# Query strips in the even layer, expert panels parted by contraction, and one panel queued ahead of a barrier

## The chip, the cores and the metric

The kernel runs on one core of one Trainium2 chip. The metric is device time in microseconds (us) of one execution. The inputs lie in the chip's main memory (HBM), and the outputs are written back there.

## The reference

Two layers of a decoder trunk are computed for 256 prompt tokens and 8 sequences of 4 new tokens, 288 tokens in all, in f32. Layer 0 ("even") is gated linear attention in chunks of 16 tokens beside a pooling mixer; layer 1 ("odd") is retention. Each mixer is followed by a mixture of 64 experts, of which every token takes 8. The two parts that the change touches are these (cut from the reference):

```python
# even layer, one chunk of 16 tokens: state query plus attention inside the chunk
q_in = qc * jnp.exp(b)
k_in = kc * jnp.exp(-b)
o_inter = jnp.einsum('bchk,bhkv->bchv', q_in, S)
att = jnp.einsum('bthk,bshk->bhts', q_in, k_in)      # then masked to s <= t
o_intra = jnp.einsum('bhts,bshv->bthv', att, vc)
S_new = jnp.exp(b_last[:, 0])[..., None] * S + jnp.einsum('bshk,bshv->bhkv', k_dec, vc)
return S_new, o_inter + o_intra

# experts: w_exp_gate and w_exp_up are 1024 x 256, w_exp_down is 256 x 1024
h = jax.nn.silu(xt @ wg) * (xt @ wu)
acc = acc + gcol[:, None] * (h @ wd)
```

The even layer has 4 heads with keys of 64 and values of 128, so a chunk's state is 64 x 128 for each head. Each new sequence has a state of its own.

## The kernel before, in words

**Even layer.** Features lie on the partitions. The queries `QI` are stored with two heads to a set of 128 partitions: for f (pair of heads) and k (head of the pair) the 64 rows of head k hold the query and the other 64 hold zeros, so one matmul against a state pair `SS[:, f, i, :]` (two heads stacked, 128 x 128) answers for one head at a time. L901 does this for the 15 chunks that have an earlier state: the state is the stationary operand (128 x 128, loaded anew for each matmul) and 32 query columns move past it (2 heads x 16 tokens). L907 does it for the 8 sequences' states `gs0` with 8 moving columns each. Both accumulate into the PSUM banks of the groups `oT` (prompt) and `oTs` (samples), which stay open while L912 (the pooling mixer's `pool` groups) runs; L919 and L924 then add the attention inside the chunks (`V` against the masked scores `AT`) and close them. L931 sums squares for the norm, and L1158, L1162 and L1116 are the output projection behind it. ScalarE copies `oT` and `oTs` out (L1541, L1450).

**Banks.** `group_order` lists every PSUM group of the program; `plan_groups` gives them the 8 banks in turn (7 in turn in the odd layer), and around the expert loop by a fixed table. A group waits until the group before it in its bank has been copied out.

**Weight panels.** The SP queue loads weights in panels of 2 MB into a ring of 6 slots (`wait_slot`, `expert_panel`). For a pair of experts panel 0 holds gate and up of the first expert, panel 1 those of the second, panel 2 the down weights of both. One pair, the last of the 32 (`HOME`), is loaded ahead of the loop into its own place in the arena (`HOME_UP`, `HOME_DOWN`) and computed in the middle of the loop, as the 17th; it is called the parked pair here. The first two pairs fill the ring before the loop. Between them the queue also issues the router's weights (`WR`), the parked pair's gate and up, then waits for a barrier of the four compute engines (`phase_end`, L750), and loads `PIN` (the layer's embedding input), the shared expert's down weights (`WSD`) and the rest of the ring.

**Expert loop.** For each pair PE does gate and up (`gate_up`, L1252, 16 matmuls, the two experts in the two column halves of the array), transposes the next pair's token rows (L1245), scatters the last pair's outputs (L1228, L1224), transposes the hidden values (L1259) and does down (L1266). Gate and up wait for panels 0 and 1 both. Panel 0 and 1 of the pair after next are issued when `gate_up` has ended (`bank_full[0]`), since they take the same slots. The token rows of each pair are gathered by an indirect DMA from `x_rows`.

## Time and profile before

| | us |
|---|---|
| median of 3 runs | 1671.39 (1671.09 to 1671.58) |
| the profiled execution's own time | 1670.99 |
| its span, first to last instruction | 1669.2 |
| PE busy in the span | 1587.6 (95%) |
| PE weight loads (PEld) busy | 799.2 (48%) |
| VectorE (DVE) busy | 539.7 (32%) |
| ScalarE (ACT) busy | 341.4 (20%) |
| GpSimd (POOL) busy | 144.6 (9%) |
| mean granted TensorE clock, share of full | 0.983 |

The chain of work that ended last is made up of PE for 81% of the span, DMA for 11%, DVE for 3%. The expert loops take about two thirds of the span: the first runs from 210 to 699 us, the second from 1129 to 1616 us.

A row of a window reads: start:end, its length, then the busy time and the count of instructions of PE, PEld, DVE, ACT and POOL, then the granted clock of PE (1.00 is full), the mean busy share of the 16 DMA engines, and the GB/s that they moved. A row of a timeline reads: start in us, duration in us, engine, line of the kernel, operation, output <- input, shapes, count (x), and in brackets how long the engine had been idle before it and who ended the wait. SPq is the queue of SyncE that issues DMAs; its duration is the issuing alone. A matmul in f32 shows as two records, so 30 matmuls are x60. A row of DMA issues ends in the median time from issue to landing.

### The profile page before, as it was taken

The page shows a single profiled execution, that of the slowest core. Times are in us where ns is not written, and L with a number is a line of the kernel's source. Part 1 is how long each engine was busy: PE and PEld are TensorE (multiplying, and loading weights), DVE is VectorE, ACT ScalarE, POOL GpSimd, SP SyncE. Part 2 cuts the span into 40 slices and gives each one's busy share as a digit, 9 for nine tenths or more (in the row PEclk, how much of TensorE's full clock was granted, in tenths as well). Part 3 has the DMA queues.
Part 4 walks back from the last instruction along what each step waited for, and adds up shares of the span by engine and source line. Part 5 has one row for each costly group of instructions (what it writes and reads, how often), then busy time and mean ns, then how long its engine had stood idle before and what let it go on. Part 6 is the DMA issues. An engine that isn't in the chain of part 4 may idle for free.

```text
span 1669.2 us, 21844 instructions
## 1 busy us (share of the span) xinstructions
PE 1587.6 (95%) x7954; PEld 799.2 (48%) x7954; DVE 539.7 (32%) x1322; ACT 341.4 (20%) x693; POOL 144.6 (9%) x221
## 2 busy tenths in 40 slices
PE   8999899999999999999999999989999999999998
PEld 5784544334344433446665755554443434443343
DVE  2145722222222222261434245372222222222225
ACT  2102122121122221231222222012212112221122
POOL 0330100000000000000011111010000000000000
PEclk9969999999999999999999999989999999999999
DMA  9623779999989999955385586577999998999970
GB/s 299 245 82 133 277 313 419 421 421 420 420 348 421 420 420 420 388 200 188 134 269 195 196 279 235 202 310 306 421 421 421 420 419 362 420 421 419 421 291 29
DMA packets 119271, 536.09 MB, mean 321 GB/s; under 512 B 17849, under 2 KB 29369, under 8 KB 69408
## 3 DMA queue, kind: packets, MB, share of 16 engines
q1 hardware_dynamic: 95975, 470.35, 70.5%
q0 software_dynamic: 21360, 61.64, 10.2%
q10 hardware_dynamic: 1872, 3.22, 0.6%
q8 instruction: 44, 0.72, 0.2%
q14 instruction: 20, 0.16, 0.0%
HBM read 526.15 MB, written 23.87 MB: 330 GB/s over the span
## 4 chain that ended last, share of the span: by engine, by line
PE 81%; DMA 11%; DVE 3%; issue 2%; ACT 1%; SPq 1%; POOL 0%; ACTq 0%; DVEq 0%
PE ps L1252 23%; PE ps L1116 12%; PE ps L1094 12%; DMA weights<-in_w_exp_up 11%; PE ps L1266 10%; PE ps L1228 5%; PE ps L1245 3%; PE ps L1224 2%; PE ps L1259 1%; PE ps L1010 1%; PE ps L1105 1%; PE ps L1286 1%; PE ps L988 1%; PE ps L901 1%; PE ps L1001 1%
## 5 line engine op out<-in xcount | busy, mean ns | idle before, releaser
L1252 PE MATMUL ps<-weights,x_feat 128*64 128x512 f32 x1984 | 437.8, 593 | 36.8 <-DMA weights<-in_w_exp_up 18.5
L1252 PEld LDWEIGHTS ps<-weights,x_feat 128*64 128x64 f32 x1984 | 147.1, 137 | 320.9 <-issue 318.2
L1266 PE MATMUL ps<-weights,arena 128*64 128x512 f32 x992 | 226.5, 598 | 0.9 <-ACT arena L1450 0.9
L1094 PE MATMUL ps<-x_feat,weights 128*128 128x288 f32 x832 | 210.2, 411 | 1.1 <-ACT x_feat L1450 1.1
L1094 PEld LDWEIGHTS ps<-x_feat,weights 128*128 128x128 f32 x832 | 159.9, 194 | 45.1 <-issue 3.8
L2104 DVE CAST split<-state 128x1024 fp32r<-128x1024 f32 (+1 forms) x66 | 44.7, 678 | 324.9 <-ACT state L1450 324.9
L2101 DVE SCALAR_TENSOR_TENSOR arena<-arena,ps 128x256 f32<-128x256 f32 x64 | 30.7, 480 | 365.3 <-ACT arena L1679 365.3
L2423 POOL DMA_INDIRECT arena<-x_rows,arena x64 | 63.6, 993 | 891.0 <-DVE arena L2094 845.9
L1450 ACT ACTIVATE state<-ps 128x512 f32<-128x512 f32 x132 | 78.8, 597 | 268.5 <-PE ps L1266 261.1
L1116 PE MATMUL ps<-weights,x_feat 128*128 128x512 f32 x288 | 126.7, 594 | 3.0 <-ACT x_feat L1476 3.0
L1266 PEld LDWEIGHTS ps<-weights,arena 128*64 128x64 f32 x992 | 65.7, 136 | 132.3 <-issue 130.9
L1679 ACT ACTIVATE arena<-ps 128x256 f32<-128x256 f32 x64 | 24.5, 383 | 444.6 <-PE ps L1252 444.6
L1228 PE MATMUL ps<-split,token_rows 128*128 128x512 f32 x256 | 111.8, 437 | 1.6 <-DVE y_low L2107 1.6
L1450 ACT ACTIVATE arena<-ps 128x256 f32<-128x256 f32 (+7 forms) x150 | 59.0, 405 | 222.4 <-PE ps L1116 84.5
L1228 PE MATMUL ps<-y_low,token_rows 128*128 128x512 f32 x256 | 100.8, 394 | 0.0
L1116 PEld LDWEIGHTS ps<-weights,x_feat 128*128 128x128 f32 x288 | 54.1, 190 | 69.8 <-issue 64.5
L1245 PEld LDWEIGHTS ps<-const,arena 128*128 128x128 f32 x512 | 62.3, 194 | 51.1 <-issue 51.1
L1116 PE MATMUL ps<-weights,arena 128*128 128x512 f32 x192 | 84.3, 592 | 0.0
L1450 ACT ACTIVATE x_feat<-ps 128x512 f32<-128x512 f32 x137 | 74.0, 588 | 49.8 <-PE ps L1245 45.9
L2107 DVE TENSOR_TENSOR y_low<-state,split 128x1024 fp32r<-128x1024 f32 (+1 forms) x66 | 78.7, 1193 | 2.3
L1245 PE MATMUL ps<-const,arena 128*128 128x128 f32 x512 | 74.4, 288 | 0.0
L1116 PEld LDWEIGHTS ps<-weights,arena 128*128 128x128 f32 x192 | 36.1, 190 | 41.6 <-issue 41.1
(289 smaller groups left out, 1280.8 us busy)
## 6 DMA issues: line engine op xcount, KB each, us to landing
weights<-in_w_exp_gate SPq DMA_DIRECT2D x124, 1024.0 KB, 14.8
weights<-in_w_exp_up SPq DMA_DIRECT2D x124, 1024.0 KB, 18.8
weights<-in_w_exp_down SPq DMA_DIRECT2D x124, 1024.0 KB, 16.9
weights<-in_w_in_c SPq DMA_DIRECT2D x24, 1024.0 KB, 8.1
arena<-in_state_ret POOLq DMA_DIRECT2D x20, 512.0 KB, 5.5
out_ret_sample<-arena POOLq DMA_DIRECT2D x20, 512.0 KB, 6.5
weights<-in_w_in_a SPq DMA_DIRECT2D x8, 1024.0 KB, 10.9
weights<-in_w_ple_gate SPq DMA_DIRECT2D x8, 1024.0 KB, 17.8
```

What stands on the lines that cost most here:

```text
L1094: last = pe.matmul(ps[:, 0:T], lhs(c), XT[:, c, :], start=(c == 0), stop=(c == n - 1))
L1116: last = pe.matmul(ps[0:r, 0:w], lhs(c), rhs(c), start=(c == 0), stop=(c == n - 1))
L1224: last = pe.matmul(PS[TS * q:TS * q + TS, 7, 0:256], TOK[u][:, SEQ:T].bitcast(F32), YF[:, 256 * q:256 * q + 256], start=False, stop=stop, ...
L1228: last = pe.matmul(bank((f"sum{l}", j, n)), TOK[u][:, P * j:P * j + P], y[:, 512 * n:512 * n + 512], start=False, stop=stop and y is YLO, ...
L1245: last = pe.transpose(ps[:, c * P:c * P + P], xc[:, 4 * q + c, :], ident)
L1252: last = pe.matmul(ps[64 * s:64 * s + 64, :], XGT[u][:, c, 64 * s:64 * s + 64], rhs, start=(c == 0), stop=(c == KC - 1))
L1266: last = pe.matmul(ps[64 * s:64 * s + 64, :], HT[u][:, c, 64 * s:64 * s + 64], wd[s][:, c, 512 * n:512 * n + 512], start=(c == 0), stop=(c ...
L1450: return act.activation(dst, src, ACT.Copy, **k)
L2101: return STT(HH[u], HS[u], META[u][:, 0:1], PS[:, 0, DE:2 * DE], ALU.mult, ALU.mult)
L2104: return dve.tensor_copy(YHI[:, c], YF[:, c])
L2107: return TT(YLO[:, c], YF[:, c], YHI[:, c].bitcast(F32), ALU.subtract)
L2423: pool.indirect_dma_start(XG[u], None, xd, bass.IndirectOffsetOnAxis(ap=GI[u], axis=0), bounds_check=last_row, oob_is_err=False).then_inc( ...
```

## The change

Three edits are made together.

1. **Query strips.** The roles in the state query are swapped: a chunk's 32 query columns are the stationary operand and the state moves past it, 128 columns. Four chunks write the four 32-row strips of a bank (L923 for the prompt, 16 chunks with the first one's state zeroed by a new memset; L930 for the 8 sequences, whose stationary columns hold the tokens of 4 sequences, 3 of them masked later). ScalarE copies three banks out (`QS` in `state`, `QSS` in `keys`, the latter scaled by the mask column `own_strip`). New matmuls turn them back to feature order and add them to `oT` (L949, against the identity) and `oTs` (L959, against `fold_all`, which sums the strips). `QI` is laid out by chunks, and three groups (`qS` twice, `qSs`) join `group_order`, so every later group's bank moves on by three.
2. **Panels parted by contraction.** For the first pair and the last pair of each loop, panel 0 holds the first half of the contraction (rows of gate and up) of both experts and panel 1 the second half (`contraction_panel`; 4 KB a piece where it was 8 KB). `gate_up_halves` waits for panel 0 alone, does 8 of the 16 matmuls, then waits for panel 1. After the first pair's first half it raises `half_consumed`, and the queue waits for that instead of for the end of `gate_up` before it issues the third pair's panel 0.
3. **One panel ahead of the barrier.** The second pair's panel 0 is issued before the queue's wait for `phase_end`, instead of behind it, `PIN` and `WSD`.

PE's program in the even layer: L901 and L907 are the state queries, L912 the pooling, L919 and L924 the attention, L931 the norm. Before:

```order
L855 MATMUL ps<-arena,side 64x128 x32
L901 MATMUL ps<-arena 128x2x16 x30
L907 MATMUL ps<-arena,ln_rows 128x2x4 x16
L912 MATMUL ps<-arena 128x288 x4
L919 MATMUL ps<-x_feat,arena 128x128 x8
L924 MATMUL ps<-x_feat,arena 128x32 x4
L931 MATMUL ps<-x_feat,small 128x512 x2
```

And the same place now (L877 is the former L855, L936 the former L912, L966 the former L931):

```order
L877 MATMUL ps<-arena,side 64x128 x32
L923 MATMUL ps<-arena 32x128 x32
L930 MATMUL ps<-ln_rows,arena 32x128 x16
L936 MATMUL ps<-arena 128x288 x4
L944 MATMUL ps<-x_feat,arena 128x128 x4
L949 MATMUL ps<-const,state 128x4x2x16 x4
L944 MATMUL ps<-x_feat,arena 128x128 x4
L949 MATMUL ps<-const,state 128x4x2x16 x4
L954 MATMUL ps<-x_feat,arena 128x32 x4
L959 MATMUL ps<-const,arena 128x2x16 x4
L966 MATMUL ps<-x_feat,small 128x512 x2
```

46 matmuls with a 128 x 128 stationary operand have become 48 with a 128 x 32 one, and 12 that turn the results have been added in front of the norm.

SP's queue between the parked pair's panels and the loop, first layer. Before, the panel of the second pair stands behind the barrier's wait, `in_p_prompt` and `in_w_sh_down`:

```order
L734 DMA arena<-in_w_exp_gate 128x2048
L734 DMA arena<-in_w_exp_up 128x2048
L622 DMA arena<-in_p_prompt 128x2x256 [waits phase_end]
L623 DMA arena<-in_p_sample 32x256
L755 DMA state<-in_w_sh_down 128x1024
L755 DMA arena<-in_w_sh_down 128x1024
L734 DMA weights<-in_w_exp_gate 128x2048 [waits bank_full_7]
L734 DMA weights<-in_w_exp_up 128x2048
L734 DMA weights<-in_w_exp_gate 128x2048 [waits bank_full_7]
L734 DMA weights<-in_w_exp_up 128x2048
```

Now:

```order
L738 DMA arena<-in_w_exp_gate 128x2048
L738 DMA arena<-in_w_exp_up 128x2048
L738 DMA weights<-in_w_exp_gate 128x2048 [waits bank_full_2]
L738 DMA weights<-in_w_exp_up 128x2048
L626 DMA arena<-in_p_prompt 128x2x256 [waits phase_end]
L627 DMA arena<-in_p_sample 32x256
L768 DMA state<-in_w_sh_down 128x1024
L768 DMA arena<-in_w_sh_down 128x1024
L738 DMA weights<-in_w_exp_gate 128x2048 [waits bank_full_2]
L738 DMA weights<-in_w_exp_up 128x2048
```

Two transfers of 1 MB each have moved ahead of the wait for the barrier; the bank that the slot's wait names is another one because the banks moved on by three.

SP's queue at the head of the loop now (before, the first transfer here waited for `bank_full_0` too, inside a counted loop):

```order
L782 TENSOR_LOAD small [waits flag_ready]
L782 ISA x2
L738 DMA weights<-in_w_exp_gate 128x2048 [waits half_consumed]
L738 DMA weights<-in_w_exp_up 128x2048
L738 DMA weights<-in_w_exp_gate 128x2048 [waits bank_full_0]
L738 DMA weights<-in_w_exp_up 128x2048
L738 DMA weights<-in_w_exp_down 128x2048 [waits bank_full_1]
```

Only the third pair's panel 0 has the new wait; its panels 1 and 2 wait as before.

The diff, cut to its core:

```diff
             g.extend(("dS", 2, f, i) for f in range(2) for i in range(2))
+            g.extend((("qS", 0), ("qS", 1), ("qSs",)))
+            g.extend(("pool", f) for f in range(4))
             g.extend((("oT", 0), ("oT", 1), ("oTs",)))
-            g.extend(("pool", f) for f in range(4))
...
+                def contraction_panel(num, e0, k):
+
+                    s = slot_full[num % SLOTS]
+                    dst = wp(num).rearrange("p (s m x) -> p s m x", s=2, m=2)
+                    for m, w in enumerate((A["w_exp_gate"], A["w_exp_up"])):
+                        src = w[l, e0:e0 + 2].rearrange("e (p c) n -> p e (c n)", c=KC)
+                        sp.dma_start(dst[:, :, m, :], src[:, :, 1024 * k:1024 * k + 1024]).then_inc(s, 16)
+
...
+                        if NUM[(f"shgu{l}",)] + 5 == n0 + 3 * pr + k:
                             sp.wait_ge(phase_end, 4 * (2 * l + 1))
...
                         wait_slot(n0 + 3 * pr + k)
-                        expert_panel(n0 + 3 * pr + k, 2 * pr, k)
+                        if pr == 0 and k < 2:
+                            contraction_panel(k + n0, 0, k)
+                        else:
+                            expert_panel(n0 + 3 * pr + k, 2 * pr, k)
...
-                def two_pairs(it, late):
-                    for u in range(1 if isinstance(it, int) else 2):
+                def two_pairs(it, late, pairs=2):
+                    for u in range(pairs):
                         for k in range(3):
                             if k == 2:
                                 sp.wait_ge(bank_full[1], base[1] + 3 * (u - 1 + late) + 6 * it)
+                            elif isinstance(it, int) and it == 1 and u + k == 0:
+                                sp.wait_ge(sem("half_consumed"), l + 1)
                             else:
                                 sp.wait_ge(bank_full[0], base[0] + 2 * (u + late) - 3 + 4 * it)
-                            expert_panel(n0 + 3 * u + k, 4 * it + 2 * u, k)
-
-                with sp.Fori(1, HOME // 2 + 1) as it:
+                            if isinstance(it, int) and it > 1 and k < 2:
+                                contraction_panel(n0 + 6 * it + k, 4 * it, k)
+                            else:
+                                expert_panel(n0 + 3 * u + k, 4 * it + 2 * u, k)
+
+                two_pairs(1, 0, 2)
+                with sp.Fori(2, HOME // 2 + 1) as it:
                     two_pairs(it, 0)
                 with sp.Fori(HOME // 2 + 1, PAIRS // 2 - 1) as it:
                     two_pairs(it, 1)
-                two_pairs(PAIRS // 2 - 1, 1)
+                two_pairs(PAIRS // 2 - 1, 1, 1)
...
+            pe.wait_ge(sem("const_in"), 16)
             for f in range(2):
-                out2 = begin(("oT", f)).rearrange("p (k t) -> p k t", k=2)
-                outs.append(out2)
-                for i in range(1, NCA):
-                    pe.matmul(out2[:, :, CA * i:CA * i + CA], SS[:, f, i, :], QI[:, f, :, CA * i:CA * i + CA],
-                              start=(i == 1), stop=False, skip_group_check=True)
-            out4 = begin(("oTs",))[:, 0:H * TS].rearrange("p (h t) -> p h t", h=H)
+                ps = begin(("qS", f))
+                for i in range(NCA):
+                    q, g = i % 4, i // 4
+                    last = pe.matmul(ps[TS * q:TS * q + TS, P * g:P * g + P], QI[:, f, i].rearrange("p k c -> p (k c)"), SS[:, f, i, :],
+                                     start=(g == 0), stop=(g == 3), skip_group_check=True)
+                end(last, ("qS", f))
+            ps = begin(("qSs",))
             for f in range(2):
                 for i in range(NSEQ):
-                    c = DSEQ * i
-                    pe.matmul(out4[:, 2 * f:2 * f + 2, c:c + DSEQ], gs0[:, f, i, :], QI[:, f, :, SEQ + c:SEQ + c + DSEQ],
-                              start=(f == 0 and i == 0), stop=False, skip_group_check=True)
+                    q, g = i % 4, 2 * f + i // 4
+                    last = pe.matmul(ps[TS * q:TS * q + TS, P * g:P * g + P], QI[:, f, NCA + i // 4].rearrange("p k c -> p (k c)"), gs0[:, f, i, :],
+                                     start=(g == 0), stop=(g == 3), skip_group_check=True)
+            end(last, ("qSs",))
...
+                out2 = begin(("oT", f)).rearrange("p (k t) -> p k t", k=2)
                 for k in range(2):
                     h = 2 * f + k
                     for j in range(2):
-                        last = pe.matmul(outs[f][:, k, P * j:P * j + P], V[:, j, P * h:P * h + P],
-                                         AT[:, h, P * j:P * j + P], start=False, stop=(k == 1 and j == 1),
-                                         skip_group_check=True)
+                        pe.matmul(out2[:, k, P * j:P * j + P], V[:, j, P * h:P * h + P], AT[:, h, P * j:P * j + P],
+                                  start=(k == 0 and j == 0), stop=False, skip_group_check=True)
+                emptied(pe, ("qS", f))
+                for g in range(4):
+                    tokens_of = out2[:, :, 64 * g:64 * g + 64].rearrange("p k (i c) -> p i k c", c=CA)
+                    last = pe.matmul(tokens_of, QS[f][:, P * g:P * g + P], ident, start=False, stop=(g == 3),
+                                     skip_group_check=True)
                 end(last, ("oT", f))
+            out4 = begin(("oTs",))[:, 0:H * TS].rearrange("p (h t) -> p h t", h=H)
             for h in range(H):
-                last = pe.matmul(out4[:, h, :], V[0:TS, 2, P * h:P * h + P], AT[0:TS, h, SEQ:T],
-                                 start=False, stop=(h == H - 1), skip_group_check=True)
+                pe.matmul(out4[:, h, :], V[0:TS, 2, P * h:P * h + P], AT[0:TS, h, SEQ:T], start=(h == 0), stop=False,
+                          skip_group_check=True)
+            emptied(pe, ("qSs",))
+            for f in range(2):
+                for g in range(2):
+                    last = pe.matmul(out4[:, 2 * f:2 * f + 2, CA * g:CA * g + CA], QSS[:, P * (2 * f + g):P * (2 * f + g) + P],
+                                     fold_all[:, 0:TS], start=False, stop=(f == 1 and g == 1), skip_group_check=True)
             end(last, ("oTs",))
...
+                def gate_up_halves(u, ring, it, ps):
+                    for k in range(2):
+                        n = ring + k
+                        pe.wait_ge(slot_full[n % SLOTS], 32 * (n // SLOTS + 1) + 32 * it)
+                        w = wp(n).rearrange("p (s m c n) -> p s m c n", s=2, m=2, c=4)
+                        for c in range(4):
+                            for s in range(2):
+                                last = pe.matmul(ps[64 * s:64 * s + 64, :], XGT[u][:, 4 * k + c, 64 * s:64 * s + 64],
+                                                 w[:, s, :, c, :], start=(k == 0 and c == 0), stop=(k == 1 and c == 3))
+                        if it == 0 and k == 0:
+                            last.then_inc(sem("half_consumed"), 1)
+                    return last
...
-                        else:
+                        elif not (first or last):
                             for n in range(ring, ring + 2):
                                 pe.wait_ge(slot_full[n % SLOTS], 32 * (n // SLOTS + 1) + 32 * it)
                         pe.wait_ge(bank_free[0], base[0] + uses(0, pr, 0))
-                        gate_up(u, HOME_UP if home else [wp(ring), wp(ring + 1)], PS[:, 0, :]).then_inc(bank_full[0], 1)
+                        if first or last:
+                            gate_up_halves(u, ring, it, PS[:, 0, :]).then_inc(bank_full[0], 1)
+                        else:
+                            gate_up(u, HOME_UP if home else [wp(ring), wp(ring + 1)], PS[:, 0, :]).then_inc(bank_full[0], 1)
...
+                    for f in range(2):
+                        full(act, ("qS", f))
+                        st.free(copy(QS[f], bank(("qS", f))), ("qS", f))
+                    full(act, ("qSs",))
+                    act.wait_ge(sem("even_table"), 16)
+                    st.free(copy(QSS, bank(("qSs",)), scale=own_strip), ("qSs",))
...
+            st.run(pool.memset(SS[:, :, 0, :], 0.0))
+            st.after
```

## Rows read from the trace of the kernel before

**Rows 1.** Windows in the first expert loop: engines, PEclk, DMA share, GB/s.

```profile
350.00:400.00 50.00, 46.02 (x244) 20.10 (x241) 11.87 (x32) 9.95 (x20) 2.97 (x3) 1.00 1.02 421
```

**Rows 2.** Timeline of the SP queue, first expert loop: weight panels issued.

```profile
217.32 0.35 SPq L734 DMA_DIRECT2D weights<-in_w_exp_gate  x1
...
223.68 0.80 SPq L734 DMA_DIRECT2D weights<-in_w_exp_down  x2
...
230.71 0.33 SPq L734 DMA_DIRECT2D weights<-in_w_exp_gate  x1
...
245.26 0.33 SPq L734 DMA_DIRECT2D weights<-in_w_exp_gate  x1
...
318.37 0.33 SPq L734 DMA_DIRECT2D weights<-in_w_exp_gate  x1
...
447.32 0.33 SPq L734 DMA_DIRECT2D weights<-in_w_exp_gate  x1
```

**Rows 3.** Timeline of PE, first and last pair of the expert loops.

```profile
210.05 7.09 PE L1252 MATMUL ps<-weights,x_feat 128*64 128x512 f32 x32 [1.13 <-ACT x_feat L1450]
...
681.64 7.09 PE L1252 MATMUL ps<-weights,x_feat 128*64 128x512 f32 x32 [1.62 <-issue]
...
1598.93 7.09 PE L1252 MATMUL ps<-weights,x_feat 128*64 128x512 f32 x32 [1.49 <-issue]
```

**Rows 4.** Windows: DMA before the loop's first panel and beside the parked pair.

```profile
212.00:216.00 4.00, 4.00 (x20) 1.56 (x18) 0.00 (x0) 0.00 (x0) 0.00 (x0) 1.00 0.00 0
...
472.00:476.00 4.00, 4.00 (x20) 1.15 (x16) 0.12 (x1) 0.00 (x0) 0.00 (x0) 1.00 0.16 65
```

**Rows 5.** Timeline of PE, the even layer's state queries and what follows.

```profile
103.69 13.01 PE L901 MATMUL ps<-arena 128*128 128x32 f32 x60
116.51 6.97 PE L907 MATMUL ps<-arena,ln_rows 128*128 128x8 f32 x32
123.33 4.19 PE L912 MATMUL ps<-arena 128*128 128x288 f32 x8
127.31 2.75 PE L919 MATMUL ps<-x_feat,arena 128*128 128x128 f32 x16
130.00 1.07 PE L924 MATMUL ps<-x_feat,arena 32*128 32x32 f32 x8
131.00 2.21 PE L931 MATMUL ps<-x_feat,small 128*128 128x512 f32 x6
```

**Rows 6.** Windows: PEclk in those queries, behind them, and in the output projection.

```profile
100.00:105.00 5.00, 5.00 (x43) 4.67 (x39) 2.18 (x12) 0.00 (x0) 0.00 (x0) 0.50 0.00 0
...
125.00:130.00 5.00, 5.00 (x23) 4.17 (x21) 1.99 (x4) 0.79 (x2) 0.00 (x0) 0.60 0.00 0
...
133.00:161.00 28.00, 28.00 (x71) 12.69 (x71) 15.74 (x18) 2.65 (x5) 0.00 (x0) 1.00 0.48 191
```

**Rows 7.** Timeline of PE at full clock: strips, wide matmuls, transposes.

```profile
47.89 1.96 PE L1111 MATMUL ps<-weights,x_feat 128*32 128x128 f32 x64
...
79.47 7.93 PE L1094 MATMUL ps<-x_feat,weights 128*128 128x288 f32 x32
...
160.51 1.04 PE L1082 MATMUL ps<-const,x_tok 128*128 128x128 f32 x8
```

**Rows 8.** The second layer's barrier: windows, SP timeline, DMA issues, PE timeline.

```profile
1085.00:1090.00 5.00, 1.70 (x10) 0.95 (x8) 3.79 (x10) 1.36 (x5) 0.00 (x0) 0.81 0.69 285
...
1090.32 0.38 SPq L622 DMA_DIRECT2D arena<-in_p_prompt  x1
...
arena<-in_p_prompt SPq DMA_DIRECT2D x1, 256.0 KB, 2.6
...
1098.15 0.74 PE L1186 MATMUL ps<-const,arena 128*128 128x128 f32 x4
```

**Rows 9.** Timeline of PE and DVE behind the first layer's shared matmuls.

```profile
198.54 0.32 PE L1216 MATMUL ps<-arena 128*128 128x12 bf16 x3 [0.55 <-DVE arena L2083]
...
199.01 0.44 DVE L2052 TENSOR_TENSOR arena<-arena,ps 128x288 f32<-128x288 f32 x1
```

More of the change, by code:

```diff
@@ L130, in constants @@
             ((p[:, None] // DSEQ) == np.arange(8)[None, :]) * 1.0,
-            np.tile(inv.reshape(-1), (P, 1))]
+            np.tile(inv.reshape(-1), (P, 1)), (p[:, None] % CA // DSEQ == p[:, None] // TS) * 1.0]
     f = np.float32
@@ L399, in trunk @@
         invc = ce.take(64)
+        own_strip = ce.take(1)
         gate_ops = a.take(8 * RANK + 256 + T)
@@ L413, in trunk @@
         EB = a.take(2 * T).rearrange("p (f t) -> p f t", f=2)
-        QI = a.take(4 * T).rearrange("p (f k t) -> p f k t", f=2, k=2)
+        QI = a.take(4 * T).rearrange("p (f i k c) -> p f i k c", f=2, k=2, c=CA)
         EN = LX
@@ L430, in trunk @@
         AT = XTb[:, 4 * T:8 * T].rearrange("p (h t) -> p h t", h=4)
+        QS = [STATE[:, 512 * f:512 * f + 512] for f in range(2)]
+        QSS = keys[:, 0:512]
         a = Cut(AR[:, :], ASZ)
@@ L887, in even_pe @@
                 for j, (o, r) in enumerate(CH):
-                    last = pe.matmul(ps[0:r, o:o + r], KI[:, h // 2, o:o + r], QI[:, h // 2, h % 2, o:o + r],
-                                     start=True, stop=True)
+                    last = pe.matmul(ps[0:r, o:o + r], KI[:, h // 2, o:o + r],
+                                     QI[:, h // 2, o // CA:(o + r) // CA, h % 2, :], start=True, stop=True)
                 end(last, ("att", h))
@@ L895, in even_pe @@
             pe.wait_ge(sem("even_in"), 16 * 8)
-            outs = []
+            pe.wait_ge(sem("const_in"), 16)
             for f in range(2):
-                out2 = begin(("oT", f)).rearrange("p (k t) -> p k t", k=2)
-                outs.append(out2)
-                for i in range(1, NCA):
-                    pe.matmul(out2[:, :, CA * i:CA * i + CA], SS[:, f, i, :], QI[:, f, :, CA * i:CA * i + CA],
-                              start=(i == 1), stop=False, skip_group_check=True)
-            out4 = begin(("oTs",))[:, 0:H * TS].rearrange("p (h t) -> p h t", h=H)
+                ps = begin(("qS", f))
[5 more added lines that the diff above has]
+            ps = begin(("qSs",))
             for f in range(2):
                 for i in range(NSEQ):
-                    c = DSEQ * i
-                    pe.matmul(out4[:, 2 * f:2 * f + 2, c:c + DSEQ], gs0[:, f, i, :], QI[:, f, :, SEQ + c:SEQ + c + DSEQ],
-                              start=(f == 0 and i == 0), stop=False, skip_group_check=True)
+                    q, g = i % 4, 2 * f + i // 4
+                    last = pe.matmul(ps[TS * q:TS * q + TS, P * g:P * g + P], QI[:, f, NCA + i // 4].rearrange("p k c -> p (k c)"), gs0[:, f, i, :],
+                                     start=(g == 0), stop=(g == 3), skip_group_check=True)
+            end(last, ("qSs",))
             for g in range(4):
@@ L1792, in even_dve @@
                         dve.wait_ge(sem("queries_zeroed"), 1)
-                    st.run(STT(QI[0:64, f, 0, :], ps[0:64], DKA ** -0.5, EB[0:64, f, :], ALU.mult, ALU.mult))
-                    st.free(STT(QI[64:128, f, 1, :], ps[64:128], DKA ** -0.5, EB[64:128, f, :], ALU.mult, ALU.mult), ("qk", f))
+                    for k in range(2):
+                        rows = slice(64 * k, 64 * k + 64)
+                        ins = STT(QI[rows, f, :, k, :], ps[rows].rearrange("p (i c) -> p i c", c=CA), DKA ** -0.5,
+                                  EB[rows, f, :].rearrange("p (i c) -> p i c", c=CA), ALU.mult, ALU.mult)
+                        if k:
+                            st.free(ins, ("qk", f))
+                        else:
+                            st.run(ins)
                 else:
```

## Prediction

> **What bounds the kernel now.** I read the granted clock and the chain of waits first, then windows, then the timeline beside each edit. PE is busy for 95% of the span and holds 81% of the chain, with DMA next at 11%, so an edit is worth what it takes off PE's path, or what it takes off a transfer that PE waits for. Three stages matter.
>
> The expert loop has two regimes. In a DMA-bound window the engines move 421 GB/s at a share of 1.02, and PE is busy for 46.02 of 50 us [rows 1]. Early in the loop a pair takes 245.26 - 230.71 = 14.6 us, since PE sets the pace; from 318.37 to 447.32, eight pairs, a pair takes 16.1 us, since the transfers do [rows 2]. A panel of 2 x 1024 KB takes 2.10 MB / 421 GB/s = 5.0 us, three panels 15.0, and the other 1.1 us are left for the token rows that each pair gathers. So the loop starts with a lead of full slots, eats it up, and then waits for DMA; what starts the transfers earlier ends the first half earlier. At the parked pair the engines run dry (share 0.16 from 472 to 476) [rows 4]: the ring is full there, and the second half starts afresh, relative to PE. A gain before the parked pair is then a plain shift of all that follows, and the second half ends DMA-bound again: the last gate-and-up waits 1.62 us in layer 0 and 1.49 in layer 1 [rows 3].
>
> The even layer's state queries are PE's alone: L901 to the start of L931 take 131.00 - 103.69 = 27.3 us without a gap [rows 5], at a granted clock of 0.50, the lower of the two levels (1.2 GHz); it is back at 1.00 before 130 [rows 6].
>
> **Part 1, query strips.** Removed: 60 + 32 = 92 records, 13.0 + 7.0 = 20.0 us, 217 ns each [rows 5]. L907 moves only 8 columns and still takes 217 ns, so the load of 128 x 128 is what is paid. Added: 32 + 16 matmuls, 96 records of four-strip form. The trace has that form in L1111: 64 records in 1.96 us at full clock, 31 ns each, that is four strips side by side [rows 7]. 96 records are 2.9 us at full clock, 5.9 at half. Then the pooling: 4.19 us as before at half clock, or 8 x 248 ns = 2.0 at full [rows 5, 7]. Then 16 records of `V` against `AT` and 16 that turn `QS` back: 130 ns each at full clock [rows 7], 4.2 us, or 6.9 at half. Then L924's 8 records, 1.07, and 8 for `QSS` at 130 ns, together 2.1. ScalarE's three copies lie behind the strips and beside the pooling, where ScalarE is idle (no busy time from 100 to 105, 0.79 us from 125 to 130) [rows 6]; without that cover they would cost about 2 us.
>
> What is left is the clock. The mean of 0.60 from 125 to 130 means a rise at about 129, 5.7 us after the 288-column matmuls began at 123.33, while 20 us of 32- and 8-column matmuls before them left it at 0.50 though PE was fully busy [rows 5, 6]. If the strips (128 columns and all four column groups at work) count like wide matmuls, the clock is back when they end, and the stage takes 5.9 + 2.0 + 4.2 + 2.1 = 14.2 us, a gain of 13.1. If only the pooling counts, it is back at 109.6 + 5.7 = 115.3: pooling until 113.8, 7 records at half clock until 115.3, 25 at full (3.3), then 2.1, end at 120.7, a gain of 10.3. I take the middle, 11.7 us. Bounds: everything at full clock is 11.2 us, a gain of 16.1; strips that don't overlap at all at half clock (96 x 217 ns = 20.8) with the same late rise end at 135.6, a loss of 4.6.
>
> [...]
>
> Everything behind shifts with L931: the norm, the output projection (28.0 us of unbroken PE work from 133 to 161 [rows 6]), the barrier.
>
> **Part 2, first pair.** `half_consumed` comes half of 7.09 us after 210.05, so the third pair's panel 0 is issued at 213.8, where it was 217.32 [rows 2, 3]. The engines are idle there (share 0.00 from 212 to 216) [rows 4]. Panel 0 then ends 3.5 us earlier, and panel 1, issued at 217.3, follows without a gap (until 223.8, with the gathered rows 225.0). Panel 2 is issued at 223.68, in time, and runs until about 230.0. The next panels come only with the end of the second gate-and-up at 230.71, so about 0.8 us of the lead is lost. That leaves 3.5 - 0.8 = 2.7 us for each layer, seen from the time on at which the loop waits for DMA: 5.4 in all. Bounds: 0 (if it is lost somewhere in the ring) and 3.5 for each layer. The matmuls themselves are the same 16.
>
> **Part 2, last pair.** PE is free at 681.64 - 1.62 = 680.0, and panel 1 lands at about 681.6, so panel 0 has landed at 676.6. The first half can start at 680.0 and PE runs on through: 1.62 us saved in layer 0, 1.49 in layer 1 [rows 3], 3.1 in all. Pieces of 4 KB where there were 8: no row shows their rate alone; even 0.5 us more a panel would put panel 1 at 682.6 and the end at 682.6 + 3.5 = 686.1, still ahead of the 687.1 that PE needs. Bounds: 0 and 3.1.
>
> **Part 3, the panel ahead of the barrier.** In layer 0 DMA waits for nothing there and nobody waits for the panel: no gain. In layer 1 the panel takes its place behind the parked pair's, which keep the engines busy until about 1088.5 (share 0.69 of 1085 to 1090), so it runs until 1093.5. `PIN`, issued at 1090.32 and landed 2.6 us later until now, is behind it and lands at about 1096.1; PE wants it at 1098.15 [rows 8]. Cost 0; if the cover of 2.0 us is gone, up to 3 us. I take 0.
>
> **Moved banks.** Every group after the new three has another bank. In layer 0 the first `lists` group now follows the last shared-expert group directly in bank 0. Its matmul started at 198.54; the copy that frees the bank ends at 199.45 [rows 9], so PE and the first gather behind it come about 1 us later. In layer 1 the same conflict (on the second list) existed before and goes. I take +1.0 - 0.8 = 0, between -1 and +2.
>
> **Sum.** Against the profiled execution's own 1670.99: -11.7 - 5.4 - 3.1 + 0 = 1650.8; that execution was 0.4 below the median of the runs, so the forecast is 1651 us. By the bounds alone it would go from 1643 to 1681.
>
> **The rivals.**
> - *Strips slow or clock late.* The four strips don't overlap as in L1111, since here each also has another stationary operand, or the clock stays at half through the turning matmuls (6.9 and about 4 instead of 4.2 and 2.1). Even layer -3 instead of -11.7: 1660. For it: 20 us of busy PE did not raise the clock. Against: L1111's 31 ns, and the rise after 5.7 us of wide matmuls.
> - *The ring eats the early start.* The DMA-bound stretch is long, and a lead may vanish where slots come free late. Then only the last pair's 3.1 is left of the loops: 1656. Against: eight pairs in a row at 16.1 us leave no slack in which to lose it.
> - *More than forecast.* Full clock within the strips, and the whole 3.5 us in each loop: -16.1 - 7.0 - 3.1, 1645.
> - *Slower: the clock stays down in the output projection.* Should the denser, shorter stage leave the clock at 0.50 until the layer norm, the 28.0 us of PE work from 133 to 161 at full clock [rows 6] would double: -3 - 8.5 + 28, 1688. It decides from about 20 us of doubled work on. For it: PE at 0.50 for some 25 us while fully busy. Against: the 288-column matmuls are still there, and 512-column ones follow.
>
> **How the numbers follow.** Forecast (both parts, 1647 to 1654) 0.66; strips slow or clock late 0.12; ring 0.11; more than forecast 0.07; slower 0.02; a mix that ends near no change 0.02. The range 1646 to 1657 holds the forecast, the ring and half of the larger gain. Within 0.2% (3.3 us, about what a measurement of this kernel can tell from no change): 0.02; faster 0.95; slower 0.03.
>
> **What would show it.** PE's strips: 96 records in 3 to 6 us, L931's successor starting 10 to 13 us earlier, at about 119. The clock's rise between 108 and 116. SP's first loop panel 3.5 us after the first gate-and-up's start, and the first half of the loop shorter by 2.7 us. No DMA wait ahead of the last gate-and-up. In layer 1 no idle time of PE before the transposes of `PIN`. The prediction is wrong if the strips take over 10 us, if the distance from the first to the parked pair is unchanged, or if PE waits for `PIN`.

## The result, and the profile after

The kernel after takes 1657.34 us (median of 4 runs, 1656.74 to 1660.54); the kernel before, run beside it, 1671.24 (1670.63 to 1671.58). The ratio is 0.9921, with a 95% interval of 0.9904 to 0.9938. The forecast was 1651 with a range of 1646 to 1657: the direction was right, the forecast gain was too large by 6 us, and the time lies 0.3 us outside the range.

The page of the kernel after (busy us, share of the span, instructions; then q8, the DMA queue that fetches PE's code as shown below, with packets, MB and share):

```profile
span 1655.4 us, 21804 instructions
...
PE 1575.6 (95%) x7982; PEld 789.3 (48%) x7982; DVE 539.4 (33%) x1322; ACT 343.7 (21%) x696; POOL 144.9 (9%) x222
...
q8 instruction: 44, 0.72, 0.2%
```

**Even layer.** Timeline of PE; it answers to [rows 5]:

```profile
103.72 3.64 PE L923 MATMUL ps<-arena 128*32 128x128 f32 x64
107.13 1.93 PE L930 MATMUL ps<-ln_rows,arena 128*32 128x128 f32 x32
108.99 2.37 PE L936 MATMUL ps<-arena 128*128 128x288 f32 x8
111.20 1.05 PE L944 MATMUL ps<-x_feat,arena 128*128 128x128 f32 x8
...
114.87 1.07 PE L954 MATMUL ps<-x_feat,arena 32*128 32x32 f32 x8
115.87 1.08 PE L959 MATMUL ps<-const,arena 128*128 128x32 f32 x8
116.78 2.18 PE L966 MATMUL ps<-x_feat,small 128*128 128x512 f32 x6
```

Windows of the same stretch (PEclk follows POOL's busy time); they answer to [rows 6]:

```profile
100.00:105.00 5.00, 5.00 (x61) 4.57 (x61) 2.58 (x15) 0.00 (x0) 0.00 (x0) 0.50 0.01 3
105.00:109.00 4.00, 4.00 (x79) 3.35 (x69) 3.15 (x13) 1.19 (x2) 0.25 (x1) 0.50 0.01 2
109.00:113.00 4.00, 4.00 (x29) 3.58 (x26) 2.03 (x4) 0.69 (x1) 4.00 (x7) 0.95 0.60 122
```

From the first state query to the norm it was 27.31 us, now it is 116.78 - 103.72 = 13.06. The granted clock, still 0.50 up to 109, is back when the strips end.

**Loops.** SP's queue at the first loop's head; it answers to [rows 2]:

```profile
199.06 0.33 SPq L738 DMA_DIRECT2D weights<-in_w_exp_gate  x1
...
202.50 0.33 SPq L738 DMA_DIRECT2D weights<-in_w_exp_gate  x1
...
209.01 0.80 SPq L738 DMA_DIRECT2D weights<-in_w_exp_down  x2
...
215.88 0.33 SPq L738 DMA_DIRECT2D weights<-in_w_exp_gate  x1
```

PE's gate and up of the 17th pair (the parked one) and of the last pair, layer 0, then of the last pair of layer 1; they answer to [rows 3]:

```profile
436.76 7.04 PE L1287 MATMUL ps<-arena,x_feat 128*64 128x512 f32 x32
...
662.58 7.04 PE L1298 MATMUL ps<-weights,x_feat 128*64 128x512 f32 x32
...
1585.16 7.04 PE L1298 MATMUL ps<-weights,x_feat 128*64 128x512 f32 x32
```

The first gate and up starts at 195.38 (210.05 before, -14.67), the 17th at 436.76 (454.68, -17.92), the last at 662.58 (681.64, -19.06) and without a wait. Up to here everything is as forecast or better.

**Behind the first loop.** PE's timeline of the kernel before, the last scatter of the loop and the output projection behind it:

```profile
698.88 0.39 PE L1228 MATMUL ps<-y_low,token_rows 128*128 128x512 f32 x1
699.11 7.03 PE L1116 MATMUL ps<-weights,arena 128*128 128x512 f32 x16
706.04 1.16 PE L1082 MATMUL ps<-const,x_tok 128*128 128x128 f32 x8
```

The same place in the kernel after:

```profile
679.78 0.40 PE L1263 MATMUL ps<-y_low,token_rows 128*128 128x512 f32 x1
685.03 9.38 PE L1151 MATMUL ps<-weights,arena 128*128 128x512 f32 x16 [4.86 <-issue]
694.33 1.16 PE L1117 MATMUL ps<-const,x_tok 128*128 128x128 f32 x8
```

PE stands still for 4.86 us where it had no gap, and "issue" says that the profile shows nothing that it waited for. Then the same 8 matmuls (16 records) take 9.38 us instead of 7.03. The windows of the kernel after show why:

```profile
680.00:685.00 5.00, 0.18 (x1) 0.00 (x0) 1.20 (x3) 0.00 (x0) 0.00 (x0) 0.78 1.07 355
685.00:690.00 5.00, 4.97 (x7) 2.18 (x8) 0.00 (x0) 0.60 (x1) 0.00 (x0) 0.54 0.96 322
690.00:695.00 5.00, 5.00 (x17) 2.35 (x16) 0.97 (x2) 3.21 (x5) 0.00 (x0) 1.00 1.01 365
```

In the idle time the granted clock fell towards its lower level (1.2 GHz), and it is back at full by 690, after PE had resumed at 685. The shift of -19.10 (679.78 against 698.88) has become -11.71 (694.33 against 706.04): 7.4 us are lost here.

Beside the gap stands a packet of code. Behind the loop PE jumps over the block for overfull experts (`pe.If(go > 0)`). These inputs never run it; it has some 250 instructions, if a matmul in f32 is counted as four (its two records and their two weight loads). Between that jump and the gap's end, queue q8 moves 16 KB. Its packets around the loop's end stand in the windows 652 to 654, 682 to 684 and 684 to 686 in the kernel after:

```profile
q8 instruction: 1, 0.02, 3.4%
...
q8 instruction: 1, 0.02, 3.4%
...
q8 instruction: 1, 0.02, 3.1%
```

and at 678.1 and 702.0 in the kernel before. Ahead of the loops such a packet comes every 170 to 317 records of PE, weight loads included (10 packets and 2,402 records up to 255.4 us, kernel before). So q8 feeds PE, and a packet (0.72 MB / 44 = 16 KB) is taken here as a page of code of about 250 instructions.

### The profile page after: what moved, and what is told of

Same layout as the page of the kernel before. It is cut to its first block, busy times and chain, and to the rows that moved or that the text cites. A ratio compares the mean times of both kernels' runs of the same rounds, so it can differ in the third digit from the quotient of the medians.

```text
span 1655.4 us, 21804 instructions
## 1 busy us (share of the span) xinstructions
PE 1575.6 (95%) x7982; PEld 789.3 (48%) x7982; DVE 539.4 (33%) x1322; ACT 343.7 (21%) x696; POOL 144.9 (9%) x222
## 4 chain that ended last, share of the span: by engine, by line
PE 83%; DMA 10%; DVE 3%; issue 2%; ACT 1%; SPq 1%; POOL 0%; ACTq 0%; DVEq 0%
PE ps L1287 22%; PE ps L1151 13%; PE ps L1129 12%; PE ps L1314 11%; DMA weights<-in_w_exp_up 10%; PE ps L1263 6%; PE ps L1280 3%; PE ps L1259 2%; PE ps L1298 2%; PE ps L1307 1%; PE ps L1045 1%; PE ps L1140 1%; PE ps L1334 1%; PE ps L1023 1%; PE ps L1036 1%
## 5 line engine op out<-in xcount | busy, mean ns | idle before, releaser
L1287 PE MATMUL ps<-weights,x_feat 128*64 128x512 f32 x1856 | 409.7, 593 | 27.6 <-DMA weights<-in_w_exp_up 14.6
L1287 PEld LDWEIGHTS ps<-weights,x_feat 128*64 128x64 f32 x1856 | 140.3, 137 | 291.0 <-issue 286.5
```

Of the source, the lines that this page charges most:

```text
L1287: last = pe.matmul(ps[64 * s:64 * s + 64, :], XGT[u][:, c, 64 * s:64 * s + 64], rhs, start=(c == 0), stop=(c == KC - 1))
```

## The experiments

There were two theories at the start. *Code*: PE waits for its own instructions at the jump's target, since 14 more matmuls in the even layer have moved the places where pages of code end. *Transfer*: PE waits for the projection's panel, issued at 655.32, or for a semaphore, as a consequence of the earlier panels.

**1. The blocks left out.** In the kernel after, for SP, PE, ACT and DVE:

```diff
-                with pe.If(go > 0):
+                if False:
```

> The kernel after, without the four blocks that compute experts with more tokens than fit (one for each of SP, PE, ACT and DVE, behind each expert loop; with these inputs the flag is 0 and the blocks are jumped over). Left out is that work and the jump. Theory (code): behind the first loop PE waits 4.9 us for its own instructions beyond the jump (685.03, released by nothing that the profile shows) and the low clock that follows costs 2.3 us more. Without the blocks there is nothing to jump over, so the stage from the end of the last down (680.2) to the end of L1151 is about 7 us shorter, the gap is under 1 us, and the whole kernel takes about 1650 us. Rival (transfer): PE waits for the panel of the projection, issued at 655.3; then the gap stays at 4 to 5 us and the time at 1657.

Measured: 1650.71 us (one run; before 1669.68 beside it). The last scatter starts at 681.34, and the projection follows it without a gap and at full speed:

```profile
681.57 7.03 PE L1151 MATMUL ps<-weights,arena 128*128 128x512 f32 x16
```

The projection's panel is issued at 656.86 here, 24.5 us ahead of the last scatter as in the kernel after, and PE doesn't wait for it. So the transfer theory is out, unless the block did something else as well.

**2. Empty instructions.** `for _ in range(64): pe.nop()` at the head of PE's program.

> The kernel after with 64 empty instructions at the start of PE's program, where PE waits for its inputs anyway; all that follows lies 64 instructions later in memory. Theory (code): where the instruction fetch falls relative to the jump sets the stall, so the 4.9 us ahead of L1151 change by more than 1 us (vanish, or grow), and the time with them (1650 if they vanish). Rival (transfer or a semaphore): 4.9 us as before, 1657.

> The kernel after with 128 empty instructions at the start of PE's program. Theory (code): the stall ahead of L1151 differs from 4.9 us in this kernel or in the one with 64, and may appear behind the second loop instead. Rival (transfer or a semaphore): 4.9 us in both, 1657.

> The kernel before with 56 empty instructions at the start of PE's program, about as many as the change adds to PE ahead of the first loop's end. Theory (code): the growth of PE's program alone brings the stall, so a gap of about 5 us appears ahead of the output projection of the first layer's experts (L1111 or its neighbour, 699.1 in the kernel before, without a gap there), and the time is about 7 us over that of before, 1678. Rival (transfer or a semaphore, a consequence of the earlier panels): no gap, 1671.

Measured: 1658.92 us with a gap of 4.83; 1657.88 with 4.70; 1671.72 without a gap. By the words of the expectations these times spoke for the rival, but the runs test nothing. q8's first packet comes after 83 or 84 matmul records in all of them (27.8 to 28.5 us), as it does in the kernels without them, so the empty instructions took no room in the code that ran. The three are repeats of before and after, and used as such below.

**3. Real instructions.** 14 or 16 matmuls of one row and one column at PE's start, while it waits for x:

```diff
             pe.wait_ge(sem("ident_in"), 16)
+            for _ in range(14):
+                pe.matmul(PS[0:1, 7, 0:1], ident[:, 0:1], ident[:, 0:1], start=True, stop=True)
```

> The kernel before with 14 matmuls of one column and one row at PE's start, where it waits for x (about 56 instructions, as many as the change adds). Theory (code page): a gap of about 4.9 us appears behind the first loop, ahead of the output projection, which then runs at half clock for some microseconds; the fetch of a page that stood at 678.1 comes about 7 us earlier, and another right after the gap; in all about 1671 + 7 = 1678. Rival: no gap, 1671.

> The kernel after with 16 matmuls of one column and one row at PE's start, where it waits for x (64 instructions). Theory (code page): the jump over the block now stands beyond a page's end and the page of its target is asked for in time, so the gap of 4.9 us and the half clock after it go: about 1657.3 - 7.3 = 1650. Behind the second loop there is no gap either (its jump stands some 150 instructions into a page, then 220). Rival: the gap stays, 1657.

Measured: the kernel before with 14 takes 1676.83 us (one run; 1670.9 without). q8's first packet now comes at 20.4 instead of 27.8, again behind 83 matmul records if those of the 14 are counted, so these do take room. The gap is there:

```profile
703.38 9.34 PE L1116 MATMUL ps<-weights,arena 128*128 128x512 f32 x16 [5.54 <-issue]
```

The kernel after with 16 takes 1650.55 us (4 runs, 1649.73 to 1650.88), ratio to before 0.9883, interval 0.9867 to 0.9900. No gap and no half clock:

```profile
681.07 0.40 PE L1265 MATMUL ps<-y_low,token_rows 128*128 128x512 f32 x1
681.31 7.03 PE L1151 MATMUL ps<-weights,arena 128*128 128x512 f32 x16
688.25 1.16 PE L1117 MATMUL ps<-const,x_tok 128*128 128x128 f32 x8
```

So adding useless work makes the changed kernel 6.8 us faster, and about as much of it makes the old one 5.9 us slower.

**4. The length of code that never runs.** The block on PE made longer in the kernel before, shorter in the kernel after (where 12 matmuls that gather rows and 4 of the down product are left out of the overflow path):

```diff
+                            rows(0, 0, PS[:, 1, :])
                             rows(0, 0, PS[:, 1, :])
...
+                            down(0, 0, halves_of(last_panels[2]), PS[:, 0, :])
                             down(0, 0, halves_of(last_panels[2]), PS[:, 0, :])
```

> The kernel before with the block that is jumped over 64 instructions longer on PE (16 matmuls more, none of them executed). What runs is the kernel before, instruction for instruction. Theory (code page): the target of the jump moves past a page's end that PE has not asked for, so a gap of 4.5 to 5.5 us and half clock after it appear behind the first loop: about 1671 + 7 = 1678. Rival (the 14 matmuls of the padded kernel acted through time, clock or a bank, not through their place): no gap, 1671.

> The kernel after with that block 64 instructions shorter on PE (16 matmuls of the experts' overflow path are left out, which these inputs don't use). What runs is the kernel after. Theory (code page): the target lies within the page that PE has asked for, the gap of 4.9 us and the half clock after it go: about 1650. Rival: the gap stays, 1657.

Measured: 1675.50 and 1650.85 us, one run each; the kernel before takes 1670.31 beside them, but with runs from 1668.59 to 1674.77, so the gap in the trace decides here and not the time. The longer block in the kernel before:

```profile
702.11 9.51 PE L1116 MATMUL ps<-weights,arena 128*128 128x512 f32 x16 [5.18 <-issue]
```

The shorter one in the kernel after:

```profile
679.62 0.40 PE L1263 MATMUL ps<-y_low,token_rows 128*128 128x512 f32 x1
679.85 7.03 PE L1151 MATMUL ps<-weights,arena 128*128 128x512 f32 x16
```

What PE executes is unchanged in both; only the target's place is moved. This is the cleanest pair, and it settles the cause. The expectation for the two slowed kernels was 1678, and they came 1.2 and 2.5 us under it. From the last gate and up of layer 0 to the first of layer 1 they take 454.40 (14 matmuls) and 454.25 (longer block) where before takes 447.59, so the stall costs 6.7 to 6.8; the rest was won ahead of it, where the first gate and up stands at 209.12 and 208.52 against 210.05 and the way to the 17th is 0.8 us shorter.

The packets agree: with a gap, q8's last one ahead of it is asked for when PE has already reached the jump (682.1 in the kernel after, 699.3 with the longer block), and a second follows 3 to 6 us later (685.4, 705.2), when PE enters the page. Without a gap the target's page had come in time (678.1 before, 670.9 with the 16 matmuls), and the packet behind the jump (702.0, 683.4) is already that of the page after it. With the shorter block a packet comes at 682.0, the same time as in the kernel after, and PE, busy in the projection, doesn't wait for it: it isn't the packet that stalls PE but the need of what it brings.

**5. The parts alone.** Part 1 without parts 2 and 3, and parts 2 and 3 without part 1; the edits are those of the diff.

> Part 1 alone (query strips; the panels and the queue as in the kernel before). It adds 14 matmuls, about 56 instructions, to PE's program in the even layer. Theory (code page: a page of 16 KB of PE's instructions, taken as 256 of 64 bytes, is fetched when PE enters the one before it; the jump over the unused block spans about one page, so its target lies one page too far when the jump stands near a page's end): the stall of 4.9 us and the clock at half after it appear in this kernel, so -14.2 in the even layer, +7.3 behind the first loop, +1.3 at the odd layer's start: about 1666 against 1671.4. Rival (the stall comes of the earlier panels or what the queue does at the loop's end): no gap behind the first loop, and 1658.

> Parts 2 and 3 alone (panels by contraction, one panel ahead of the barrier; the even layer as in the kernel before). PE gets no matmul more. Theory (code page): no gap behind the first loop; the gain is what the loops gave in the kernel after, 3.2 and 1.7 ahead of the parked pairs, 1.6 and 1.7 at the last pairs: -8.2, about 1663. Rival (the stall comes of the panels): a gap of 4.9 us behind the first loop, and 1670.

Measured: strips 1666.03 us (10 runs), ratio 0.9979 (0.9969 to 0.9988), with the gap:

```profile
688.36 8.79 PE L1133 MATMUL ps<-weights,arena 128*128 128x512 f32 x16 [4.54 <-issue]
```

Panels 1664.88 us (6 runs), ratio 0.9964 (0.9951 to 0.9976), without a gap (694.96, 7.03 us). The stall comes with the strips' instructions, not with the panels. By the medians the strips alone are worth 4.9 us. The profiled run, at 1663.49 the fastest of ten (up to 1669.53), shows 7.5: -15.2 at the first gate and up, and +7.6 between the last gate and up of layer 0 and the first of layer 1. Why the ten spread by 6 us no trace shows. The panels' 6.0 us are 2 short of the expectation (1663): in the trace the two loops give 7.7, the first gate and up stands 0.6 later than before, and 1.1 is lost between the layers, where the clock is down for longer (below).

**6. The panels' edits, undone one at a time, in the kernel with the 16 small matmuls.**

```diff
-                            elif isinstance(it, int) and it == 1 and u + k == 0:
-                                sp.wait_ge(sem("half_consumed"), l + 1)
```

> The kernel after with the 16 small matmuls at the start (1650.6), but the third pair's first panel waits for the end of the first gate and up again, as before; the panels stay parted by contraction. Theory: this wait alone carries the first pair's gain; from the first gate and up to the 17th takes 2.7 us longer in layer 0 (241.3 to 244.0, the means of six and four kernels) and 2.1 in layer 1 (240.9 to 242.9), the last pair is unchanged: about 1655.4. Rival (the other order of the rows in the panels does it): both distances as with the early issue, 1650.6.

Measured: 1653.09 us (one run). The first and the 17th gate and up, layer 0 and then layer 1:

```profile
195.07 7.09 PE L1298 MATMUL ps<-weights,x_feat 128*64 128x512 f32 x32 [1.03 <-ACT x_feat L1501]
...
438.80 7.04 PE L1287 MATMUL ps<-arena,x_feat 128*64 128x512 f32 x32
...
1112.11 7.09 PE L1298 MATMUL ps<-weights,x_feat 128*64 128x512 f32 x32 [1.03 <-ACT x_feat L1501]
...
1354.77 7.04 PE L1287 MATMUL ps<-arena,x_feat 128*64 128x512 f32 x32
```

243.7 and 242.7 us, as the theory said (244.0, 242.9): the early issue carries that gain. The total is 2.3 us under the expectation. Against the trace with the 16 matmuls, this run was 2.1 us earlier at the first gate and up and won 2.2 between the layers, both places where the clock falls in some kernels and not in others (below); its last pairs came 0.5 and 0.8 later.

```diff
-                        if NUM[(f"shgu{l}",)] + 5 == n0 + 3 * pr + k:
+                        if NUM[(f"shgu{l}",)] + 4 == n0 + 3 * pr + k:
                             sp.wait_ge(phase_end, 4 * (2 * l + 1))
```

> The kernel after with the 16 small matmuls, but the second pair's first panel is issued behind the barrier, the layer's inputs and the shared down weights again, as before (part 3 undone). Theory: part 3 is worth nothing within 0.3 us in either layer, since the ring is full ahead of the first pair in both (DMA share 0.02 from 1125 to 1133 before): 1650.6. Rival (it costs or gives something in layer 1, by PE's wait for the layer's inputs or by a later start of the loop): the first gate and up of layer 1 stands 0.5 us or more elsewhere, and the time differs by as much.

Measured: 1649.42 us (4 runs), ratio 0.9877 (0.9857 to 0.9896) beside 0.9883. Layer 1, the transposes of the gated input and the first gate and up, with the panel behind the barrier:

```profile
1071.53 1.97 PE L1117 MATMUL ps<-const,x_tok 128*128 128x128 f32 x8 [3.66 <-DVEq L595]
...
1110.69 7.09 PE L1300 MATMUL ps<-weights,x_feat 128*64 128x512 f32 x32 [1.03 <-ACT x_feat L1503]
```

and ahead of it:

```profile
1074.00 1.97 PE L1117 MATMUL ps<-const,x_tok 128*128 128x128 f32 x8 [3.67 <-DVEq L595]
...
1113.17 7.09 PE L1300 MATMUL ps<-weights,x_feat 128*64 128x512 f32 x32 [1.03 <-ACT x_feat L1503]
```

That is 39.16 and 39.17 us, and from the last gate and up of layer 0 to the first of layer 1 both take 449.32. Part 3 is worth nothing; the 1.1 us between the medians are not its own. The profiled run with the panel behind the barrier stands 2.6 us ahead at the first gate and up of layer 0 (194.57 against 197.13), 1.7 of them because the clock stayed full behind the list (below), as it did in the kernel after, which has part 3.

## Why the prediction was right and wrong

Distances between gate and up starts, from all twelve experiments and the two kernels, against the terms of the sum (in square brackets the number of kernels):

| term | forecast | measured |
|---|---|---|
| even layer, first query to norm | -11.7 | -14.25 (27.31 to 13.06) |
| first to 17th pair, layer 0 | -2.7 | -2.6 (243.9 [6] to 241.3 [8]) |
| the same, layer 1 | -2.7 | -2.0 (242.9 [6] to 240.9 [8]) |
| 17th to last pair, layer 0 | -1.6 | -1.5 (227.2 [5] to 225.7 [9]) |
| the same, layer 1 | -1.5 | -1.6 (227.2 [5] to 225.5 [9]) |
| part 3 | 0 | 0 |
| stall behind the first loop, with the half clock after it | none | +7.4 |
| clock at the odd layer's start | none | +1.2 |
| barrier to first pair | 0 | -0.4 (-14.67 at 195.38) |

Rows with a number of kernels in brackets are means over the kernels that share the form; the others are read from the traces of the two kernels themselves. They add up to -13.7, and the two profiled executions differ by 1657.38 - 1670.99 = -13.6. Without the rows of the stall, the clock and the barrier the forecast's own terms come to -22.0, where it had -20.2.

**The step that failed** is "Everything behind shifts with L931". What the runs show in its place is a stall of PE behind the first loop, 4.86 us, and 2.4 us of half clock after it: the shift of -19.10 becomes -11.71. The prediction took the 12 matmuls in front of the norm for their time alone (24 records at 130 ns, 3.1 us), and never asked what they do to the program as code, so the sum has no term for it. The trace of before held the warning, though no view ranks it: the page of the profile lists `q8 instruction`, and the diff adds 14 matmuls to PE ahead of a jump. No rival had this either; the one that came out nearest in time, the ring (1656), was wrong in its mechanism, since the loops gave 7.7 us of the 8.5 that they should.

With the stall taken out by the 16 small matmuls the kernel takes 1650.55, almost the forecast's 1651. That agreement is partly luck: in its trace the even layer gave 15.3 us, 3.6 more than forecast, and the clock behind the list and between the layers took back 1.7 us each.

The Trainium skill, "Runtime: NRT & Kernel Launch" (Instruction fetch mechanics), has the rule that speaks against this change: code comes in blocks of 16 KiB, 256 instructions, fetched in sequence, and a taken branch whose target isn't in the current window of two pages forces a fetch before execution goes on. The runs agree, with 4.5 to 5.5 us for such a fetch. The block is about one page of code long, so the jump's target mostly lies one page on, and two when the jump stands near a page's end; moving the jump or its target by 56 or 64 instructions switched the stall on in two kernels and off in two. Where the ends of pages lie is worked out from the packets' times and not read from the trace. I read that section after the result and should have before.

**Even layer: mechanism right, size too small.** The strips took 108.99 - 103.72 = 5.3 us (forecast 5.9), the pooling 2.2 (2.0), the rest 5.6 (6.3). The clock rose at about 109, at the strips' end, which was the better of my two cases (-13.1); I took the middle of the two, which neither would give. It had stayed down through 20 us of 32- and 8-column matmuls [rows 5, 6] and rose behind 5 us of strips; what makes that difference no run here isolates. The kernel after is moreover the slowest of the nine with the strips at this place: the stage takes 11.6 to 13.1 us in them. With the shorter block it takes 115.07 - 103.42 = 11.65, since the clock is back while the strips still run:

```profile
105.00:109.00 4.00, 4.00 (x78) 3.41 (x71) 3.62 (x14) 1.88 (x3) 0.54 (x1) 0.87 0.01 2
```

So the part of the rival *More than forecast* that had the full clock within the strips came true in some kernels.

**First pair.** The third pair's panel 0 was issued when expected (199.06, 3.7 us after the first gate and up began), and the next panels came at 215.88 with the end of the second gate and up, so 0.8 us of the lead was lost as worked out. Layer 0 gave the 2.7. Layer 1 gave 0.7 less; why is open. The kernels with the early issue differ among themselves by more than that (240.1 to 241.5).

**Last pair.** Right, 1.5 and 1.6: the last gate and up starts without a wait. The smaller pieces cost nothing that shows.

**Moved banks.** In layer 0 PE does wait longer for the list, as worked out. The kernel after, then the kernel after with the 16 small matmuls:

```profile
184.64 0.55 PE L1251 MATMUL ps<-arena 128*128 128x12 bf16 x6 [1.60 <-DVE arena L2115]
```

```profile
184.70 0.55 PE L1253 MATMUL ps<-arena 128*128 128x12 bf16 x6 [1.61 <-DVE arena L2117]
```

The wait was 0.55 [rows 9], so it grew by 1.05. In four of the nine kernels with the new banks the clock falls behind it as well; windows from 185 of after, where it doesn't, and of after with the 16:

```profile
185.00:190.00 5.00, 5.00 (x16) 2.34 (x15) 2.05 (x11) 0.00 (x0) 2.12 (x2) 1.00 1.00 410
```

```profile
185.00:190.00 5.00, 5.00 (x12) 2.18 (x13) 2.07 (x11) 0.00 (x0) 2.12 (x2) 0.66 0.99 417
```

That costs 1.7 us (the first gate and up stands 10.7 us behind the list in after, at 195.38, and 12.4 with the 16, at 197.13), and lies in the term's range of up to +2. Other banks for the lists might avoid it; that wasn't tried.

**The odd layer's start** is a second place of that kind, where idle time of PE ends at full or half clock. After, two windows:

```profile
737.00:742.00 5.00, 3.88 (x14) 2.80 (x13) 0.69 (x1) 0.60 (x1) 2.06 (x4) 0.54 1.05 402
742.00:747.00 5.00, 5.00 (x17) 3.78 (x17) 0.17 (x2) 0.00 (x0) 0.00 (x0) 0.78 1.01 409
```

In the kernel before the fall was shorter (0.66 from 750 to 755, then 1.00). It isn't the banks: with the banks of before, the panels alone show 0.71 and then 0.60, and before with 14 matmuls 1.00 throughout. Whether the clock falls at such a gap, and for how long, differs between kernels whose work there is the same; what decides it stays open. At two such places it moved one kernel's total against another's by up to 4.3 us (2.1 and 2.2 in experiment 6), so compare distances within a trace before totals.

## What to carry to other kernels

When a change adds or removes instructions ahead of a taken jump over a long block, look at where the page ends of that engine's code fall: compare the code packets around the jump before and after. If a gap of about 5 us with the releaser "issue" stands behind it, move the jump or its target by some dozens of instructions. A block well under a page should help too, but only one run here had a shorter one. Price a change as code as well as time. Where a sum has two cases for one term, take the likelier, not their middle, and let the other widen the range: here the better case was 1.1 us off and the middle 2.5.

## What the runs showed of the hardware

- A taken jump to a page of code that isn't there costs PE 4.5 to 5.5 us (4.54, 4.86, 5.18, 5.54; 4.70 and 4.83 in the repeats), and 1.8 to 2.6 us more since the clock is down when it resumes (the 8 matmuls take 8.79 to 9.59 us instead of 7.03). Both ends of the fetch show in the kernel after: the packet at 682.1, 2 us behind the last matmul, and PE's next instruction 2 us behind the packet's end.
- 56, 64 or 128 empty instructions at PE's start did not move the later code: here they were no padding, small matmuls were.
- The second loop has the same block and stalled in none of the thirteen kernels that have it (the projection behind it took 7.03 us in each).
- A 128 x 32 stationary operand in four strips ran at about 55 ns a record at half clock (5.27 us / 96), where the 128 x 128 one had taken 217 [rows 5].
